# Routed experts: both halves of a pair's gate and up product in one run on TensorE

## The reference

```python
N_EXPERTS = 64; TOPK_EXPERTS = 8; EXPERT_FF = 256; D_MODEL = 1024; SEQ = 256

def swiglu(x, w_gate, w_up, w_down):
    return (jax.nn.silu(x @ w_gate) * (x @ w_up)) @ w_down

def moe_ffn(xt, w_router, router_bias, w_gate_e, w_up_e, w_down_e, ...):
    # scores, group mask, top 8 of 64 experts per token, weights wts
    ...
    for e in range(N_EXPERTS):      # in effect
        rows = tokens routed to e
        routed[rows] += swiglu(xt[rows], w_gate_e[e], w_up_e[e], w_down_e[e]) * wr[:, None]
    return routed + swiglu(xt, w_gate_sh, w_up_sh, w_down_sh)
```

## Time and profile before

| | |
|---|---|
| time, 3 runs | 1452.04, 1454.57, 1466.34 us; median 1454.57 |
| profiled execution | 1460.52 us, of which the span of the instructions 1458.7 |
| PE busy | 1323.3 us, 91% of the span |
| DVE, ACT, POOL busy | 551.6, 476.8, 30.5 us |
| mean granted clock of PE | 0.949 of full |
| moved by DMA | 372.32 MB, mean 255 GB/s |
| routed stage (L1941 to the last L1977) | 327 to 866 us of the span |

### The profile page before, as it was taken

The page is one execution under the profiler, slowest core; times in us unless marked ns, Lnnn a source line. Parts: engine busy times, 40 slices in busy tenths (PEclk is TensorE's granted clock), DMA queues, the critical chain, the costliest instruction groups (busy, mean ns, idle before and its releaser), DMA issues.

```text
span 1458.7 us, 16861 instructions
## 1 busy us (share of the span) xinstructions
PE 1323.3 (91%) x6656; PEld 908.8 (62%) x6656; DVE 551.6 (38%) x735; ACT 476.8 (33%) x692; POOL 30.5 (2%) x41
## 2 busy tenths in 40 slices
PE   3799998779999999999999977999969978599996
PEld 0777777664544554454454436888859767488885
DVE  0545456643111111111111125464544653554543
ACT  1354444322222122222222224434333633434342
POOL 1000000000000000000000000030000000000000
PEclk9899999789999999999999998999989969899999
DMA  9976755568999999999999995655614204355640
GB/s 353 355 274 234 246 181 176 201 248 346 392 380 399 393 398 385 409 393 384 376 370 383 384 324 144 211 183 173 217 38 156 97 1 156 105 176 200 201 142 29
DMA packets 133529, 372.32 MB, mean 255 GB/s; under 512 B 14771, under 2 KB 62180, under 8 KB 118316
## 3 DMA queue, kind: packets, MB, share of 16 engines
q1 hardware_dynamic: 131824, 365.29, 68.5%
q10 hardware_dynamic: 1340, 2.94, 0.6%
q0 software_dynamic: 320, 3.46, 0.6%
HBM read 368.47 MB, written 4.50 MB: 256 GB/s over the span
## 4 chain that ended last, share of the span: by engine, by line
PE 85%; DVE 6%; DMA 4%; ACT 2%; issue 1%; SPq 1%; POOL 1%; POOLq 0%; ACTq 0%; DVEq 0%
PE bank L1780 28%; PE bank L1941 15%; PE bank L1873 9%; PE bank L1965 8%; PE bank L1913 4%; PE bank L1977 4%; PE bank L1834 4%; DMA ada_g<-in_w_ada 2%; DMA ring<-in_w_up_e 2%; DVE h_tok L1147 1%; PE bank L2030 1%; PE bank L2054 1%; PE bank L1796 1%; PE bank L1767 1%; PE bank L1930 1%
## 5 line engine op out<-in xcount | busy, mean ns | idle before, releaser
L1941 PE MATMUL bank<-ring,xg 128*64 128x512 f32 x1088 | 248.5, 598 | 3.4 <-DMA ring<-in_w_up_e 3.3
L1132 DVE TENSOR_TENSOR g_lo<-raw_g,g_hi 128x2048 fp32r<-128x2048 f32 (+2 forms) x88 | 201.8, 2294 | 125.8 <-ACT g_hi L723 66.3
L1780 PE MATMUL bank<-g_hi,xt_hi 128*128 128x512 f32 (+1 forms) x592 | 240.1, 406 | 4.7 <-DVE arena L1177 2.5
L1780 PE MATMUL bank<-g_hi,xt_lo 128*128 128x512 f32 (+1 forms) x592 | 233.0, 394 | 0.0
L1780 PE MATMUL bank<-g_lo,xt_hi 128*128 128x512 f32 (+1 forms) x592 | 232.3, 392 | 0.0
L1941 PEld LDWEIGHTS bank<-ring,xg 128*64 128x64 f32 x1088 | 79.4, 137 | 141.9 <-issue 133.6
L1780 PEld LDWEIGHTS bank<-g_hi,xt_hi 128*128 128x128 f32 x592 | 113.4, 192 | 33.5 <-issue 7.3
L1780 PEld LDWEIGHTS bank<-g_hi,xt_lo 128*128 128x128 f32 x592 | 112.5, 190 | 24.0
L1965 PE MATMUL bank<-ring,a_t 128*64 128x512 f32 x544 | 124.2, 598 | 3.4 <-ACT a_t L824 1.3
L1780 PEld LDWEIGHTS bank<-g_lo,xt_hi 128*128 128x128 f32 x592 | 113.3, 191 | 21.9
L1271 DVE SCALAR_TENSOR_TENSOR arena<-arena,w_row_of,bank 128x256 f32<-128x256 f32 x34 | 16.3, 480 | 242.4 <-ACT arena L820 242.4
(11 more groups left out here) (294 smaller groups left out, 1712.9 us busy)
## 6 DMA issues: line engine op xcount, KB each, us to landing
ring<-in_w_up_e SPq DMA_DIRECT2D x64, 1024.0 KB, 19.7
ring<-in_w_gate_e SPq DMA_DIRECT2D x64, 1024.0 KB, 10.8
ring<-in_w_down_e SPq DMA_DIRECT2D x32, 2048.0 KB, 18.2
raw_g<-in_ffn_w_gu SPq DMA_DIRECT2D x44, 1024.0 KB, 9.2
raw_g<-in_w_in SPq DMA_DIRECT2D x26, 1024.0 KB, 7.1
raw_d<-in_ffn_w_down SPq DMA_DIRECT2D x22, 1024.0 KB, 5.0
ada_d<-in_w_ada SPq DMA_DIRECT2D x16, 1024.0 KB, 5.1
raw_g<-in_w_out SPq DMA_DIRECT2D x8, 1024.0 KB, 5.0
```

The costliest lines, as they stand in the source:

```text
L1132: dve.tensor_tensor(lo, raw, hi.bitcast(F32), ALU.subtract).then_inc(S.lo_g, 1)
L1780: last = pe.matmul(out_, src[s][:, c, b * P:(b + 1) * P], w((g_hi, g_lo)[m], i), start=start and i == 0 and k == 0, stop=stop and i == len ...
L1941: last = pe.matmul(bank(4)[r, :].rearrange("p (g n) -> p g n", g=2), xg[:, s // 2 % 2, c, at_:at_ + ROWS], gate_up_raw(s, j, c), start=c = ...
```

## The change

On PE, `body(s)` runs both halves of the gate and up product one behind the other, and the first `fill` of the pair comes after them, directly ahead of `scatter`. On ACT, Silu, which needs both halves, is put ahead of the evacuation of that fill. The lists of DVE, SP and POOL are the same.

```diff
@@ ACT, body(s) @@
                     if s:
                         rows_down(s - 1, it)
+                    act.wait_ge(used_gu, at(4 * s + 4, it, 16))
+                    act.activation(silu[:, 0, :], bank(4)[:, 0:FF], ACT.Silu).then_inc(sp_silu, 1)
                     if more:
                         gathered(2 * s + 4, it)
-                    act.wait_ge(used_gu, at(4 * s + 4, it, 16))
-                    act.activation(silu[:, 0, :], bank(4)[:, 0:FF], ACT.Silu).then_inc(sp_silu, 1)
                     if s + 1 < N_PAIR:
                         pick_t(s + 1, it)
@@ PE, body(s) @@
-                    rows_gate_up(s, 0, it)
+                    for u in range(2):
+                        rows_gate_up(s, u, it)
                     if s == 1:
...
                     if more:
                         fill(2 * s + 4, it)
-                    rows_gate_up(s, 1, it)
                     if s:
                         scatter(s - 1, it)
```

## The result

The changed kernel takes 1443.59 us (median of 4 runs, 1441.51 to 1446.09) against 1455.07 for the kernel before (4 runs, 1452.04 to 1466.34): a ratio of 0.9883, 95% interval 0.9848 to 0.9917. In a later comparison it took 1443.54, ratio 0.9851 (0.9807 to 0.9895). It is 11.5 us faster; 2 were forecast, and the time lies just under the range of 1444 to 1463.

The account below looks back on a forecast made before the run. PE was taken to bound the stage only just, with DMA's weight stream absorbing most of PE's 9.6 us saving. Forecast: 1454.57 - 1 (profiled execution's gain) - 1 (DMA slack left) = 1452.5 us, own range 1449 to 1456, with rivals 1444 to 1463.

Parts of the forecast that it names:

- The reading of the bound: Stage of pairs 0 to 33: PE bounds it only just, 15.8 us a pair, with DMA close behind.
- DMA needs 6.29/0.391 = 16.1 us: Weight stream: a pair's 6.29 MB at the traced 391 GB/s takes longer than PE's 15.8 us.
- PE's 9.6 us do not come through: If the weight stream ends the stage, PE's saving over 32 pairs is mostly lost; 2 us less remains.
- debt of fixed growth: Down weights' landing: 9.4 us after issue growing to 25.2, 0.66 us a pair, until PE waits for the ring.
- What PE saves: Two fewer switches between 64-row and 128-row matmuls a pair: 0.30 us, 9.6 us over 32 pairs, bounds 4.5 and 11.2.
- The sum of three steps: Second half 0.16, last fill step 0.08, first scatter matmul 0.11: 0.35 us a pair from distances between starts.
- rival 1: Whole PE saving stays if DMA runs at 413 GB/s throughout: 1445 us (1443.4 to 1450), chance 22%.
- Rival 2: Deeper DMA queue blocks SP's issues and slows the stream to 367 GB/s: 1462 us, chance 14%.
- Rival 3: PE's switches cost nothing that can be removed: 1454.6 us, the same, chance 8%.
- the order of ScalarE and its cover: Silu ahead of the fill's evacuation costs nothing; its cover grows by 1.14 us; without cover, 1 us a pair.
- the earlier start of the stream: At the stage's start, an earlier second issue brings the whole weight stream forward by up to 1.1 us.
- just escapes that stall: Median run, 1454.57 us, read as missing the 5.0 us of ring waits and slow clock in the profiled execution.

Follow-up runs that it names:

- e5: Kernel before with half of the gate and up matmuls left out, all weights still loaded: 1427.31 us.
- e6: Changed kernel with half of the gate and up matmuls left out, all weights still loaded: 1422.68 us.
- e12: Kernel before, nothing changed, profiled again: span 1454.9 us, stage 537.8 us, 6.2 us of PE's waits for the ring.
- e14: Kernel before, nothing changed, profiled again: span 1450.9 us, stage 537.1 us, 5.5 us of PE's waits for the ring.
- e9: Kernel before, nothing changed, timed against itself and profiled again: 1461.51 us, stage 530.7 us, no wait for the ring.
- e7: Kernel before with the fill split within and behind the first gate/up half, six matmul-kind switches a pair instead of four: 1463.92 us, ratio 1.0012.
- e1: Changed kernel with the fill ahead of both adjoining gate/up halves (except pair 1), four switches a pair, ScalarE's old order: 1454.71 us.
- e2: Changed kernel with ScalarE's old order, the copy of the fill ahead of Silu: 1441.33 us, ratio to before 0.9867.
- e3: Kernel before with only half of the down weights loaded from pair 2 on (light stream): 1453.1 us.
- e4: Changed kernel with only half of the down weights loaded from pair 2 on (light stream): 1443.61 us.
- e13: Kernel before, nothing changed, profiled again in a long execution: span 1463.1 us, stage 543.2 us, 9.9 us of PE's waits for the ring.
- e10: Kernel before with SyncE issuing the first half's loads only when the second half is free too: 1464.28 us, ratio 1.0035.
- e11: Changed kernel with the second half of the ring slot freed by the first fill's last but one matmul: 1441.46 us.

## Why the prediction was wrong

**The reading of the bound (what bounds the kernel now) failed at one step: "DMA needs 6.29/0.391 = 16.1 us".** The rate at a busy share of 1.01 was taken for the ceiling. A share of 1 didn't mean that no more would fit: at a share of 1.02 the engines moved 412 GB/s when PE was made light (e5, e6). 391 was under the demand of 398, but it was the rate of this order in this execution, and the new order moved 404 and 407. From there "PE's 9.6 us do not come through" followed, and the forecast of 2 us.

**The growing landing times were read as a debt of fixed growth.** The debt itself is real, and its limit was read rightly: in the profiled execution and in e12 and e14 the down weights land after 25.2 to 27.0 us at 716 to 732 us, and the waits of PE begin at 742 to 758. But 0.66 us a pair was the growth in one execution and not a property of the stream: in e9, the same kernel, the landing goes from 9.4 to 17.2 us over the same time, and PE never waits. The changed kernel goes from 11.2 to 24.4 with 1.6 us of waits in one profile and from 11.9 to 15.1 with none in the other (345:361 and 764:780).

**What PE saves was right in mechanism and a little short in size.** The sum of three steps, 0.35 us a pair, was right (e7: 0.35; light stream: 0.37), in part by luck: its 0.16 set a distance between starts, 3.59, against a length in the chain, 3.43. Read alike, the first half is 3.54, and only 0.05 is left between the two; the 0.16 is right for both halves together (7.13 to 6.97). The 0.30 taken in place of the sum was too low. 32 pairs make 11.8 us of stage, not 9.6, and the range's lower end, set at rival 1's centre, was too high by that: 1443.4, the rival's own outer bound, is nearly what came. That the whole time met it so closely is luck, since the kernel before was 17.7 us over the changed one in the later comparison.

**Rival 1 (22%) is in the main what happened.** Its condition asked for 413 GB/s throughout, which was more than it took: 404 and 407 GB/s nearly keep up with a PE that wants 408. The Trainium skill, HBM Reference, section Specifications (TRN2), has about 425 GB/s for a core streaming alone and about 358 when both cores of the pair stream. The 412 measured in e5 and e6 is nearer to the first, so this rule would have led the right way.

**Rival 2 falls by e6:** blocked issues at 412 GB/s. The low rates and the blocked issues stood together in the trace, but the block by itself, the sign of a full queue, cost nothing in e6; what makes the rate fall in the old order isn't shown. **Rival 3 falls by e1 and e7.**

**Right were** the order of ScalarE and its cover (e2), that no other wait grows (one of 0.8 us in one of the two profiles apart), and the earlier start of the stream: the second half's issue follows the first gate/up matmul after 337.79 - 330.5 = 7.3 us, before after 335.85 - 327.3 = 8.6. The reading that the median run of before "just escapes that stall" was too neat: its five profiles lose 0 to 12.5 us of stage to the stream.

**How the gain is made up.** 11.8 us are PE's switches, shown by the stages of e3 and e4. The rest is what the old order loses to the stream: its stage is 537.0 us in the mean of five profiles, 6.3 over the 530.7 without a wait, and that of the changed kernel 520.05 in two, 1.2 over 518.9. By the stage the gain is 17 us, in the two comparisons of whole times 11.5 and 17.7. The long runs go with it: 11 of 23, 6 of 13, 8 of 23 and 6 of 12 runs of the kernel before took 1462 us or more in the later sessions, none of the 8 of the changed kernel came over 1446.09, and one of e2's six stood 10 us over its others.

Why the old order is open to this is not settled. Shown is that it comes from the stream (e3) and lies in the stage (e13); that e1, at the same pace of 15.8 us and the same demand, had no long run in 12, 402 GB/s where the old order had 394, and landing times that grow from 11.7 to 13.2 us only; that neither the distance of the halves' issues (e10, e11) nor a full queue alone (e6) makes it. What the old order and e10 have, and e1, the changed kernel, e2 and e11 have not, is the fill between the two halves on PE, and no run here shows how that could reach the DMA.

## What to carry to other kernels

On a PE that never waits, the order of its matmuls can still be worth something: group those of one tile shape, and read the price from the distances between starts in the timeline, where one pair of switches was 0.35 us of 15.8. Before a gain on the busiest engine is written off against a second resource, find out what that resource can do, not what it did: a busy share of 1 says that it is in use, growing latencies that it falls behind in this execution, and a kernel with the first engine's work thinned out gives its ceiling in one run. Where plain runs of a kernel spread by 1% or more, compare a stage in several profiles; the medians alone would have called the six switches free.

## What was not expected of the hardware

- DMA at a share of 1.02 moved 412 GB/s with the queue nearly always full, and 391 to 407 at shares of 1.01 and 1.02 when less was asked. At 0.93 it moved 334.
- With PE at the same pace and the same weights asked for, the place of the fill on PE changed what DMA moved in the first 155 us of the window: 394 GB/s with the fill between the halves, 402 with it ahead of them.
- A change between 64-row and 128-row matmuls and back costs PE 0.35 us: 0.11 at the first scatter matmul, 0.08 at the last fill step and 0.16 in the two narrow halves together.
- The same kernel on the same chip lost between 0 and 12.5 us of stage to a stream that fell behind (in one stretch down to 296 GB/s over 8 us) from one execution to the next, and a small change of order on PE made these all but vanish.
- Of PE's waits for the ring in the profiles of the kernel before, two were followed by a stretch at the lower of the two clock levels (1.2 in place of 2.4 GHz): 2.25 us in the profile of before (granted clock 0.57 of full from 776 to 780 us) and 1.90 us in e13 (0.59 from 732 to 736), with 5.29 and 5.28 us for 16 matmuls in place of 3.65. The length of the wait didn't decide it: one of 2.35 us in e12 was followed by full speed.

```profile
777.61 3.65 PE L1941 MATMUL bank<-ring,xg 128*64 128x512 f32 x16 [2.35 <-DMA ring<-in_w_up_e]
```
